# Key pages loaded 32 tokens at a time to all 128 partitions, instead of four heads at a time to 32 partitions

## The reference, cut to what matters

```python
k_past = cache_k[page_table].reshape(n_s, past_len, N_HEADS, HEAD_DIM)   # 8 x 2048 x 16 x 64, float32
v_past = cache_v[page_table].reshape(n_s, past_len, N_HEADS, HEAD_DIM)
s_past = jnp.einsum('nqhd,nkhd->nhqk', q, k_past).astype(jnp.float32) * ATTN_SCALE
s_past = s_past + cq - c_past.transpose(0, 2, 1)[:, :, None, :]
p = jax.nn.softmax(jnp.concatenate([s_past, s_new], axis=-1), axis=-1)
out = jnp.einsum('nhqk,nkhd->nqhd', p[..., :past].astype(v_past.dtype), v_past)
```

## Time and profile before

| | |
|---|---|
| median of 3 runs | 1722.51 us (1710.47 to 1722.52) |
| profiled execution, its own time | 1728.96 us |
| its span, first to last instruction | 1727.3 us |
| mean granted TensorE clock | 0.856 of full speed |
| PE busy (81%) | 1392.8 us |
| DVE busy (29%) | 506.4 us |
| ACT busy (17%) | 289.9 us |
| moved by DMA | 424.60 MB, 246 GB/s over the span |
| loads of key pages | 512 of 128 KB, SP's queue |

### The profile page before, as it was taken

The page is one execution under the profiler, slowest core; times in us unless marked ns, Lnnn a source line. Parts: engine busy times, 40 slices in busy tenths (PEclk is TensorE's granted clock), DMA queues, the critical chain, the costliest instruction groups (busy, mean ns, idle before and its releaser), DMA issues.

```text
span 1727.3 us, 34388 instructions
## 1 busy us (share of the span) xinstructions
PE 1392.8 (81%) x13632; PEld 972.9 (56%) x13632; DVE 506.4 (29%) x1026; ACT 289.9 (17%) x673; POOL 118.5 (7%) x176
## 2 busy tenths in 40 slices
PE   4988999997699993776676676677689579999991
PEld 3877888885345441333333333343344469888881
DVE  3330101000423223554545544544511410010002
ACT  2120100110111113232222212222220101001000
POOL 1021000000200001001000001000000020000002
PEclk8789999998799997677777678677799689999996
DMA  8267999999611316599999999999953338999975
GB/s 235 113 221 245 392 382 398 386 402 337 231 39 36 97 49 191 138 277 259 245 237 240 255 235 243 243 238 238 260 197 158 119 132 334 376 396 383 388 308 179
DMA packets 177433, 424.60 MB, mean 246 GB/s; under 512 B 32807, under 2 KB 112744, under 8 KB 168911
## 3 DMA queue, kind: packets, MB, share of 16 engines
q1 hardware_dynamic: 129751, 308.93, 55.2%
q10 hardware_dynamic: 37168, 85.02, 16.2%
q0 software_dynamic: 10448, 29.73, 5.9%
HBM read 393.73 MB, written 30.24 MB: 245 GB/s over the span
## 4 chain that ended last, share of the span: by engine, by line
PE 46%; DMA 21%; issue 16%; SPq 8%; DVE 5%; ACT 2%; ACTq 1%; POOL 1%; DVEq 0%; POOLq 0%
DMA W<-in_w_up 13%; PE PS L979 10%; PE PS L866 6%; DMA KB<-in_cache_k 6%; PE PS L862 5%; SPq L380 5%; PE PS L892 4%; PE PS L897 3%; PE PS L1163 2%; PE PS L801 2%; PE PS L1120 2%; PE PS L1065 2%; DVE KB L1958 1%; PE PS L1104 1%; PE PS L1085 1%
## 5 line engine op out<-in xcount | busy, mean ns | idle before, releaser
L862 PE MATMUL PS<-W,VB 128*32 128x384 f32 x3072 | 353.6, 492 | 16.9 <-DMA W<-in_w_up 6.3
L866 PE MATMUL PS<-W,VB 128*32 128x128 f32 x3072 | 352.9, 275 | 4.7 <-issue 4.6
L866 PEld LDWEIGHTS PS<-W,VB 128*32 128x32 f32 x3072 | 335.8, 111 | 11.1 <-issue 8.9
L892 PE MATMUL PS<-W,VB 128*32 128x384 f32 x1536 | 176.5, 496 | 5.5 <-ACT VB L1323 5.5
L1958 DVE STREAM_TRANSPOSE KB<-KB 128x1024 f32<-128x1024 f32 x128 | 158.2, 1236 | 76.4 <-DMA KB<-in_cache_k 76.2
L897 PE MATMUL PS<-W,VB 128*32 128x128 f32 (+1 forms) x1024 | 176.4, 331 | 0.0
L1765 DVE TENSOR_TENSOR VB<-VB,PS 128x384 f32<-128x384 f32 x32 | 17.7, 554 | 511.9 <-PE PS L878 470.3
L862 PEld LDWEIGHTS PS<-W,VB 128*32 128x32 f32 x3072 | 145.6, 110 | 29.3 <-DMA W<-in_w_up 12.0
L1085 PE MATMUL PS<-C,W 128*128 128x128 f32 x160 | 41.2, 368 | 111.1 <-DVE W L1986 111.1
L897 PEld LDWEIGHTS PS<-W,VB 128*32 128x32 f32 x1024 | 102.9, 111 | 16.3 <-issue 1.0
L1104 PE MATMUL PS<-W 128*64 128x128 f32 (+2 forms) x480 | 75.2, 294 | 31.8 <-ACT W L1504 22.2
(11 more groups left out here) (261 smaller groups left out, 1562.1 us busy)
## 6 DMA issues: line engine op xcount, KB each, us to landing
W<-in_w_gate SPq DMA_DIRECT2D x32, 2048.0 KB
W<-in_w_up SPq DMA_DIRECT2D x32, 2048.0 KB, 21.4
W<-in_w_down SPq DMA_DIRECT2D x32, 2048.0 KB, 11.3
KB<-in_cache_k SPq DMA_DIRECT2D x512, 128.0 KB, 9.3
W<-in_cache_v ACTq DMA_DIRECT2D x56, 512.0 KB, 9.2
VB<-in_cache_v ACTq DMA_DIRECT2D x56, 512.0 KB, 8.8
yd<-VB ACTq DMA_DIRECT2D x32, 288.0 KB, 6.9
W<-in_w_kvf SPq DMA_DIRECT2D x4, 2048.0 KB, 15.6
```

The costliest lines, as they stand in the source:

```text
L862: pe.matmul(PS[32 * q:32 * q + 32, bank, 0:WIDE], x, w[:, k, 0:WIDE], start=(k == 0), stop=(k == KC - 1), tile_position=(0, 32 * q), skip_ ...
L866: mm = pe.matmul(PS[CAP:P, bank, P * q:P * q + P], x, w[:, k, WIDE:FF], start=(k == 0 and q == 0), stop=(k == KC - 1), tile_position=(0, C ...
L892: pe.matmul(PS[32 * q:32 * q + 32, 5 + n, 0:WIDE], h, w[:, f, n * WIDE:n * WIDE + WIDE], start=(f == 0), stop=(f == FC - 1), tile_position ...
```

## The change

The four loads of a key page are cut the other way. Before, load `a` brings heads 4a to 4a + 3 of all 128 tokens into partitions 32a to 32a + 31, in four pieces for each partition. After, load `c4` brings tokens 32 c4 to 32 c4 + 31, all 16 heads, into all 128 partitions, one piece each, into columns 256 c4 to 256 c4 + 255 of the page.

```diff
                 if keys:
-                    for a in range(4):
-                        eng.dma_start(to[32 * a:32 * a + 32, :].rearrange("p (c f) -> p c f", c=4),
-                                     src[:, 256 * a:256 * a + 256].rearrange("(c t) f -> t c f", t=32)).then_inc(s, 16)
+                    for c4 in range(4):
+                        eng.dma_start(to[:, 256 * c4:256 * c4 + 256],
+                                      src[32 * c4:32 * c4 + 32, :].rearrange("t (a f) -> a t f", a=4)).then_inc(s, 16)
```

## The result

The changed kernel takes **2072.48 us** (median of 4 runs, 2063.07 to 2081.19) against 1717.39 us: ratio **1.207**, 95% interval 1.1984 to 1.2156. It is slower by some 355 us, as forecast in direction, but the forecast was 2315 us with a range from 2110.

What follows compares the result with a forecast made beforehand. Four DMA engines bound the attention loop: keys 29.2, values 6.1, bias 1.4, staging 0.9, completion writes 0.2 make 37.8 us a chunk; 30 chunks from 700 us add 590 us, forecast 2315 us, range 2110 to 2650.

Steps and rivals of the forecast that it cites:

- the second: Attention loop: key loads use all 16 engines and 128 partitions, so pieces get cheaper; 1665 to 1685 us, chance 0.04.
- Rivals 1 and 3: Loop: 1, four engines always colliding, about 2660 us, part of 0.93; 3, 16 engines but no faster, 1722 us, 0.03.
- With 57 ns: 29.2 for keys: Attention loop: 512 key pieces of 1 KB a chunk on each of four engines, 57 ns each, 29.2 us.
- The lower end, 47.5 ns: Least time for a 1 KB key piece on one engine, taken from the `pool_w` load; 24.3 us of keys a chunk.
- a fifth for engines in each other's way and for bursts of values: Key piece in the loop: raised from 47.5 to 57 ns for engines meeting in SBUF and value pieces coming as a burst.
- at most about 90 GB/s: Key loads: the most that four engines would ask for, below the 209 and 377 GB/s seen with 16.
- The lower end of the whole sum: Attention loop: keys, values, bias and staging at their lowest, 31.6 us a chunk, 2120 us in all.
- values were 6.1: Attention loop: 32 value pieces of 4 KB a chunk on each of 16 engines at 190 ns, 6.1 us.
- bias, staging and completion writes: Attention loop, a chunk on each of the four engines: bias 1.4, GpSimd's staging 0.9, completion writes 0.2 us.
- The starting point: Start of the loop: chunk 1, issued at 664.64, lands near 700 us, and 30 more chunks follow at 37.8 us.
- The loop's DMA share: Sign in the profile after: DMA share in the loop falls from 1.01 to 0.39, at some 120 GB/s.
- that sign: Sign in the profile after: a key load's time from issue to landing grows from 10.0 us to 30 us or more.

Runs made afterwards that it cites:

- e1: Changed kernel with the source reordered so both sides of a key load have 128 outermost, keys landing in other places: 1666.58 us, 0.968 of before.
- e2: Changed kernel with each key load cut in two, 64 partitions each, source 2 outermost: 2742.31 us, 1.594 of before.
- e3: Changed kernel without the loads of values in rounds 1 to 7: 1900.4 us, 1.104 of before.
- e5: Changed kernel with the bias stored four times in HBM, so that a bias load can use 16 engines: 2071.08 us, 1.206 of before.
- e9: Kernel before with a chunk's 16 key loads regrouped, groups 0 and 1 of all four pages first, then 2 and 3: 1755.99 us, 1.028 of before.
- e10: Kernel before with a chunk's 16 key loads regrouped, groups 0 and 2 of all four pages first, then 1 and 3: 1684.91 us, 0.986 of before.

## Why the prediction was wrong

**The mechanism was right.** Which stage, which engines and why: the loop is bound by the DMA engines, and the changed loads go to four of them, since their source has 4 outermost. e1 and e2 show it from both sides. Of the rivals, the price of the second came out in e1, for which 1665 to 1685 us had been worked out and 1666.58 was measured; its condition, 16 engines, isn't met by the change. Rivals 1 and 3 fall by the share of 0.28 at 98 GB/s: four engines, at full pace.

**What failed is one term of the sum, the price of a key piece: "With 57 ns: 29.2 for keys".** Measured with keys alone, a key piece takes 41.8 ns on each of the four engines, so 512 of them take **21.4 us**, 7.8 less. Two errors made it.
- The lower end, 47.5 ns (47.3 by its own working), was wrong as worked out. I divided the time by the 737 packets of `pool_w` and multiplied by the share of 1.09. The recorded times of pieces overlap on an engine (in the changed kernel's stretch of keys alone a share of 0.28 of 16 engines makes some 47 ns a piece, while a new one comes every 41.8 ns), so the share has no place in the product; the pace of an engine is its bytes in the time gone by: 377 GB/s over 16 engines, 23.6 GB/s, 43.5 ns. The bias loads said the same, 25.7 GB/s for each of four engines, 40 ns for 1 KB. So even the "lower end" lay above both rows that showed undisturbed engines.
- Then I added a fifth for engines in each other's way and for bursts of values. The pace of keys alone, 98 GB/s, leaves no room for the first of these on four engines, and it is above the "at most about 90 GB/s" of the prediction.

The lower end of the whole sum, 31.6 us a chunk and 2120 us, lay above the truth for the first reason alone (with 43.5 ns it is 29.6 us), and so did the range.

The other terms, against the runs: values were 6.1 and measured at 6.3 (e3). What is left of 30.4 us, 2.7, stands for bias, staging and completion writes, which were 2.5 together. These weren't measured one by one, and e5 shows that they are less sure than the sum looks: taking three quarters of the bias off the four engines was to give back 1 us a chunk, and gave nothing clear.

The starting point, chunk 1 landing near 700 us, was right by luck. Its first transpose, and SP's loads of chunks 2 and 3:

```profile
700.66 1.24 DVE L1958 STREAM_TRANSPOSE KB<-KB 128x1024 f32<-128x1024 f32 x1
```

```profile
698.85 41.27 SPq L380 DMA_DIRECT2D KB<-in_cache_k  x32
```

The transpose shows no wait for its keys, so they were there before its tick came. What starts the 30 chunks in a row is that SP waits for chunk 0's product until 698.85 us: (1603.67 - 698.85) / 30 = 30.2 us a chunk.

With 21.4 for 29.2 the same sum gives 30.0 us a chunk and 700 + 900 = 1600 for the last landing (1603.67 measured). That is 355.6 us more than 1244.40; added to 1729.0, less 6.5 for the median, it makes 2078 us, within 0.3% of what was measured. (The prediction's own 2319 less 6.5 is 2312.5, not 2315, which changes nothing.)

**Smaller points.** The loop's DMA share was to be 0.39 at 120 GB/s and is 0.46 at 150. The shorter chunk makes it 0.42 by the same sum; the overlap of recorded times, 0.28 for a quarter, is a likely cause of the rest. The transposes were to wait some 20 us at every chunk and wait 14.6 on the mean (365.0 us, 25 times). PE's share fell from 306.34 of 440 to 310.42 of 720 us and its granted clock from 0.72 to 0.63, at no cost, as said; it didn't halve. The profile gives no time from issue to landing for the changed key loads, so that sign can't be read. The issue of a key load does cost more, 544 ns for 317 while nothing holds it up, and that is hidden.

## What to carry to other kernels

Before reshaping a DMA, write down the outermost count of both its sides: with 128 and 4 the load ran on four engines, with 64 and 2 on two, however many partitions it filled. A stretch of the profile in which such a load is alone shows it at once, by a DMA share of 0.25. To price a transfer, take the bytes over the time gone by and over the number of engines from a stretch where it is alone; a share above 1 is no part of it. And where 32-partition loads must stay, try to issue them so that neighbours go to different halves of the partitions: here that is 1.7% for one line, better than both kernels compared.

## What the runs showed of the hardware that I had not expected

- SP's queue is held up when its DMA engines are behind: 544 ns an issue for the first six loads, later about 1.13 us each and 1.33 us from start to start, the engines' pace. In the chain of waits that reads as 32% for SP.
- The order of a chunk's 16 loads in one queue, all of the same size and spread over the same 16 engines, moves the kernel by 71 us between its worst and best form (e9 and e10).
- Four engines reach 98 GB/s on 1 KB pieces. 16 engines on loads of 32 partitions reach 209 in one stretch and 228 over the whole first chunk: twelve more engines only little more than double the pace.
- The number of packets under 512 B goes with the engines of a load, 12 fewer a load after the change, so it counts the engines without a look at the time.
- Keys and bias share the same four engines (102 GB/s together in e3), and yet putting the bias on 16 made the changed kernel no faster: 2071.08 for 2072.48 us, where 30 us were expected. Why is open.
